# An expert kernel's first item: its rows turned by one-hot products straight from memory, and its item table computed between the up chunks

## What is computed

```python
h = h + mixed @ w_out[layer]
hn = rms_norm(h, norm_ffn_g[layer])
# moe_ffn(hn):
logits = xt @ router_w + router_b            # 512 x 32
top_vals, top_idx = lax.top_k(logits, 4)
gates = jax.nn.softmax(top_vals, axis=-1)
# tokens sorted by expert, in blocks of 128 rows of one expert each
gu = xblk @ w_gate_up[e] + b_gate_up[e]      # 1024 -> 2048
gate = jnp.minimum(gu[:, 0::2], 7.0)
lin = jnp.clip(gu[:, 1::2], -7.0, 7.0)
act = gate * jax.nn.sigmoid(1.702 * gate) * (lin + 1.0)
yb = act @ w_down[e] + b_down[e]             # 1024 -> 1024
y = zeros.at[buf_tok].add(yb * buf_gate[:, None])
return h + y
```

## Time and profile before

| | before |
|---|---|
| median of 3 executions | 1493.48 us |
| profiled execution: time / span in the profile | 1492.42 / 1490.8 us |
| mean granted TensorE clock over the span | 0.967 of 2.4 GHz |
| TensorE busy | 1436.0 us, 96% |
| VectorE busy | 1267.5 us, 85% |
| ScalarE busy | 1008.8 us, 68% |
| GpSimd busy | 262.1 us, 18% |
| DMA | 445.21 MB, mean 299 GB/s |

### The profile page before, as it was taken

The page is one execution under the profiler, slowest core; times in us unless marked ns, Lnnn a source line. Parts: engine busy times, 40 slices in busy tenths (PEclk is TensorE's granted clock), DMA queues, the critical chain, the costliest instruction groups (busy, mean ns, idle before and its releaser), DMA issues.

```text
span 1490.8 us, 20013 instructions
## 1 busy us (share of the span) xinstructions
PE 1436.0 (96%) x6500; PEld 1166.0 (78%) x6500; DVE 1267.5 (85%) x1020; ACT 1008.8 (68%) x971; POOL 262.1 (18%) x280
## 2 busy tenths in 40 slices
PE   6999989888999999999999999999999999999995
PEld 4887547775888888888888888888888888888884
DVE  4594865667999999999999999999999999999994
ACT  5346464334777777777777777777777777777773
POOL 3000000045011111221121111111211111221111
PEclk9999879958999999999999999999999999999998
DMA  7421001649999999999999999999999999999971
GB/s 241 154 79 57 1 1 65 260 122 301 355 384 361 385 371 366 370 375 374 373 364 366 371 367 367 381 356 368 386 359 382 365 356 368 378 371 365 370 290 21
DMA packets 96745, 445.21 MB, mean 299 GB/s; under 512 B 14863, under 2 KB 18975, under 8 KB 63888
## 3 DMA queue, kind: packets, MB, share of 16 engines
q1 hardware_dynamic: 82752, 421.82, 74.9%
q0 software_dynamic: 11392, 17.61, 4.9%
q10 hardware_dynamic: 2576, 5.46, 1.1%
HBM read 439.43 MB, written 22.43 MB: 310 GB/s over the span
## 4 chain that ended last, share of the span: by engine, by line
PE 94%; DVE 2%; ACT 1%; DMA 1%; issue 1%; SPq 0%; POOL 0%; ACTq 0%; POOLq 0%; DVEq 0%
PE psum L1257 27%; PE psum L1259 27%; PE psum L1258 27%; PE psum L1548 2%; PE psum L1573 2%; PE psum L1557 2%; PE psum L1355 2%; PE psum L1343 1%; DMA ring<-in_w_in 1%; PE psum L1357 1%; PE psum L1582 1%; PE psum L1477 1%; PE psum L1417 1%; DVE wlo L1160 0%; PE psum L1495 0%
## 5 line engine op out<-in xcount | busy, mean ns | idle before, releaser
L1160 DVE TENSOR_TENSOR wlo<-ring,whi 128x2048 fp32r<-128x2048 f32 x384 | 871.1, 2289 | 82.2 <-ACT whi L769 78.2
L769 ACT ACTIVATE whi<-ring 128x2048 fp32r<-128x2048 f32 x384 | 736.8, 1919 | 240.5 <-PE psum L1259 240.5
L1257 PE MATMUL psum<-whi,xT_hi 128*128 128x512 f32 x1024 | 402.9, 393 | 3.9 <-DVE xT_lo L1166 2.8
L1258 PE MATMUL psum<-whi,xT_lo 128*128 128x512 f32 x1024 | 399.8, 390 | 0.0
L1259 PE MATMUL psum<-wlo,xT_hi 128*128 128x512 f32 x1024 | 399.7, 390 | 0.0
L1257 PEld LDWEIGHTS psum<-whi,xT_hi 128*128 128x128 f32 x1024 | 193.2, 189 | 44.2 <-DVE xT_lo L1166 3.6
L1259 PEld LDWEIGHTS psum<-wlo,xT_hi 128*128 128x128 f32 x1024 | 192.9, 188 | 40.4
L1258 PEld LDWEIGHTS psum<-whi,xT_lo 128*128 128x128 f32 x1024 | 193.2, 189 | 39.0
L1257 PE MATMUL psum<-whi,aT_hi 128*128 128x512 f32 x512 | 202.5, 396 | 1.9 <-ACT y_sb L792 1.9
L1259 PE MATMUL psum<-wlo,aT_hi 128*128 128x512 f32 x512 | 199.7, 390 | 0.0
L1258 PE MATMUL psum<-whi,aT_lo 128*128 128x512 f32 x512 | 199.1, 389 | 0.0
(11 more groups left out here) (248 smaller groups left out, 1417.1 us busy)
## 6 DMA issues: line engine op xcount, KB each, us to landing
ring<-in_w_gate_up SPq DMA_DIRECT2D x256, 1024.0 KB, 7.6
ring<-in_w_down SPq DMA_DIRECT2D x128, 1024.0 KB, 6.9
ring<-in_w_in SPq DMA_DIRECT2D x10, 1024.0 KB, 11.5
ring<-in_w_out SPq DMA_DIRECT2D x4, 1024.0 KB, 5.0
h<-in_x SPq DMA_DIRECT2D x4, 512.0 KB, 5.5
hn_rows<-hn ACTq DMA_DIRECT2D x4, 512.0 KB, 3.0
out<-h ACTq DMA_DIRECT2D x4, 512.0 KB, 10.6
bias_rows<-rows_st SPq DMA_DIRECT2D x1, 1280.0 KB, 4.8
```

What stands on the lines that cost most here:

```text
L769: nc.scalar.activation(whi[:, hi_of(number), :], ring[:, slot(number), :], ACT.Copy).then_inc(hi_ready, 1)
L1160: TT(wlo[:, slot(number), :], ring[:, slot(number), :], whi[:, hi_of(number), :].bitcast(F32), ALU.subtract).then_inc(lo_ready, 1)
L1257: MM(o, s_hi, m_hi, start=first, stop=False)
L1258: MM(o, s_lo, m_hi, start=False, stop=False)
```

## The change

- Item 0's rows are no longer gathered. `first_rows(t)` multiplies the rows of hn, still in SBUF, by the one-hot matrix of expert 0's slots (`sel_rows`) and adds the four tiles up in PSUM banks 6 and 7: the rows come out chosen and turned. These are f32 products of 128x128, 8 a tile.
- The ranks use fp32r copies (`tri_r`, `ones_r`, `mask_r`): one pass.
- The first slots of items 1 and 2 (8 products in place of 12), the counts, the prefix, the item table and the turned gates are issued on TensorE between the up chunks 0 to 4 of item 0. VectorE's and ScalarE's lists are reordered to match; onehj is kept for all tiles, so that place(1) to place(3) and dense_gates can come later.
- ScalarE makes the high parts of chunks 0 and 1 between its gate exponentials.
- GpSimd gathers item 1 first, then writes all 16 scatters, then (after xgT_done) clears b_hl's upper half, then gathers item 2.

The core of the diff (address lines and renamings are left out):

```diff
@@ GpSimd
-                if isinstance(n, int) and n == 0:
+                if isinstance(n, int) and n == 1:
...
             nc.gpsimd.memset(xg[:, :], 0.0).then_inc(xg_cleared, 1)
             pool.wait_ge(slot0_ready, 1)
-            gather(0, slot0_i[:, 0:1])
+            gather(1, slot0_i[:, 1:2])
+            for t in range(T):
+                scatter_rows(t)
+            pool.wait_ge(xgT_done, 2)
             nc.gpsimd.memset(b_hl[2 * E:P, :].bitcast(F32), 0.0).then_inc(bhl_pad, 1)
-            scatter_rows(0)
-            scatter_rows(1)
-            gather(1, slot0_i[:, 1:2])
-            scatter_rows(2)
-            scatter_rows(3)
             gather(2, slot0_i[:, 2:3])
@@ ScalarE
             gates_exp(1)
+            hi_item(0, 0)
             gates_exp(2)
+            hi_item(0, 1)
...
             gates_exp(3)
...
-            for k in range(FIRST_HI):
-                hi_item(0, k)
-            act.wait_ge(gdT_done, 1)
-            nc.scalar.activation(gateT[:, :, :], bank(7)[0:E, :].rearrange("p (t c) -> p t c", t=T),
-                                 ACT.Copy).then_inc(gdT_evac, 1)
+            hi_item(0, 2)
             xgT_out(0)
+            hi_item(0, FIRST_HI)
+            hi_item(0, FIRST_HI + 1)
...
             nc.scalar.activation(b_hl[0:2 * E, :], b_raw[:, :], ACT.Copy).then_inc(bhl_hi, 1)
-            for k in range(FIRST_HI, UP):
+            for k in range(FIRST_HI + 2, UP):
                 hi_item(0, k)
+            act.wait_ge(gdT_done, 1)
+            nc.scalar.activation(gateT[:, :, :], bank(4)[0:E, :].rearrange("p (t c) -> p t c", t=T),
+                                 ACT.Copy).then_inc(gdT_evac, 1)
@@ VectorE
-                COPY(mask[:, t, 1:3, :], mask[:, t, 0:1, :].to_broadcast([P, 2, E])).then_inc(mask_ready, 1)
+                COPY(mask_r[:, t, :], mask[:, t, 0, :]).then_inc(mask_ready, 1)
+                COPY(mask[:, t, 1:3, :], mask[:, t, 0:1, :].to_broadcast([P, 2, E])).then_inc(mask_copied, 1)
...
             first_slot(0)
+            choose(1)
             dense_gates(0)
-            choose(1)
-            place(1)
+            choose(2)
             first_slot(1)
-            dense_gates(1)
-            choose(2)
-            place(2)
+            lo_item(0, 0)
             first_slot(2)
             choose(3)
             first_slot(3)
+            place(1)
+            place(2)
+            split_xgT(0)
+            dense_gates(1)
             place(3)
+            lo_item(0, 1)
             dve.wait_ge(slot0_done, 1)
...
+            flags()
+            dense_gates(2)
+            dense_gates(3)
+            lo_item(0, 2)
             places()
-            lo_item(0, 0)
+            lo_item(0, 3)
             items()
-            lo_item(0, 1)
-            split_xgT(0)
-            for k in range(2, UP):
+            for k in range(4, UP):
                 lo_item(0, k)
-                if k == FIRST_HI:
+                if k == 4:
@@ TensorE
+            def first_rows(t):
+
+                pe.wait_ge(sel0_ready, AHEAD * t + 1)
+                pe.wait_ge(hn_ready, t + 1)
+                if t == 0:
+                    pe.wait_ge(h1_done, T)
+                for half in range(2):
+                    for k in range(4):
+                        d = (half * 4 + k) * P
+                        ins = MM(bank(6 + half)[:, k * P:(k + 1) * P], hn[:, t, d:d + P], sel_rows[:, t, :],
+                                 start=(t == 0 and k == 0), stop=(t == T - 1 and k == 3))
+                    if t == T - 1:
+                        ins.then_inc(xgT_done, 1)
...
             ranks(0)
+            turn_hn(2)
             logits(1)
-            turn_hn(2)
             turn_hn(3)
+            logits(2)
             ranks(1)
-            logits(2)
             logits(3)
-            first_slots_of(0)
-            first_slots_of(1)
+            first_rows(0)
             ranks(2)
-            first_slots_of(2)
+            first_rows(1)
             ranks(3)
-            first_slots_of(3)
...
+            first_rows(2)
+            first_rows(3)
+            def counts():
+                pe.wait_ge(mask_copied, T)
+                pe.wait_ge(slot0_ready, 1)
...
-            pe.wait_ge(items_ready, 1)
-            pe.wait_ge(gdT_evac, 1)
-            transpose_xg(0)
             pe.wait_ge(xgT_ready, 2)
             for k in range(UP):
                 use_up(0, k, k)
+                if k == 0:
+                    for t in range(T):
+                        first_slots_of(t)
+                if k == 1:
+                    counts()
+                if k == 2:
+                    prefix()
+                if k == 3:
+                    item_table()
+                if k == 4:
+                    turn_gates()
             pe.wait_ge(bhl_ready, 1)
             pe.wait_ge(bhl_pad, 1)
             bias_up(0)
+            pe.wait_ge(items_ready, 1)
+            pe.wait_ge(gdT_evac, 1)
```

## The result

The changed kernel takes 1499.40 us (median of 5 executions, 1499.12 to 1502.54) against 1493.43 us for the kernel before (5 executions, 1489.54 to 1494.27). The ratio is 1.0046, with a 95% interval of 1.0035 to 1.0057: the change makes the kernel 6 us slower. The forecast was 1498.5, range 1493.5 to 1505.5. The profiled execution took 1499.24 us, 6.8 more than the profiled one of before (1492.42).

The account below looks back on a forecast made before the run. TensorE was taken to bound the kernel, with 94% of the span. 1490.8 - 11.4 (front) + 13.5 (up chunks) + 4.0 (clock) = 1496.9 us of span, with 1.6 outside it 1498.5; range 1493.5 to 1505.5.

Parts of the forecast that it names:

- Part 1: Way to the first up product: it starts at 313.5 instead of 324.93 us, gain 11.4 us (8.2 to 11.9).
- The factor of four: Rival in first_rows: f32 products four times as long as turnings, first up product at 333.5, 1518.5 us; chance 0.03.
- Part 2: Up chunks of item 0: VectorE's subtractions queued behind waits leave TensorE idle; eight chunks take 38.3 us instead of 24.75.
- Part 3: Gaps before up chunks: TensorE's clock falls twice, costing 4.0 us (1.6 to 6).
- Part 4: GpSimd's clearing of b_hl behind 16 scatters ends at 352.6 to 354.1, a floor of 2.8 to 4.3 us loss, adding nothing.
- Behind bias_up(0) nothing changes its order: After the up chunks: b_down products, item 1's turning and the loop take what they took before.
- The clock staying up: Rival in the gaps between chunks: clock stays at its upper level, only the clearing's floor binds, 1496.0 us; chance 0.15.
- The faster rival: Rival in the up chunks: subtractions done ahead cover the exchanges and the clearing does not bind, 1484.8 us; chance 0.07.
- the slow scatters: Rival on GpSimd: all scatters take 2.79 us, the clearing ends at 366, +16, 1508.5 us; chance 0.08.

Follow-up runs that it names:

- e8: Changed kernel with GpSimd's clearing of b_hl early and 12, 8 and 8 unused fill products in TensorE's three gaps: 1494.90 us, ratio 1.0018.
- e1: Changed kernel with VectorE's subtractions for chunks 2, 3 and 4 one place earlier, ahead of the waits: 1500.73 us, ratio 1.0047.
- e4: Changed kernel with 16, 10 and 10 unused fill products in TensorE's three gaps: 1499.66 us, ratio 1.0037.
- e2: e1 with GpSimd's clearing of b_hl ahead of the gather and the scatters: 1488.73 us, ratio 0.9974.
- e6: e2 with dense gates and b_hl's subtraction later, subtractions ahead of every exchange, turned gates behind chunk 6, ranks(2) ahead of first_rows(0): 1484.95 us, ratio 0.9942.
- e3: Changed kernel with early clearing; first slots, counts, prefix, item table and turned gates ahead of chunk 0; subtractions 1 to 7 behind places(): 1490.74 us, ratio 0.9981.
- e10: e6 with the ranks as f32 products of two records again: 1485.83 us, ratio 0.9963.
- e11: e3 with ranks(2) ahead of first_rows(0) and b_hl's subtraction behind the last chunk's: 1490.59 us, ratio 0.9973.

## Why the prediction was right, point by point

- **Part 1, the front: right in its working, 1 us off in its figure.** The first up product came at 312.46, released by xT_lo as said, against my 313.5; that is 0.5 us below the earliest time that I gave (313.0). The gain is 12.5 us, not 11.4. The last of first_rows ended at 311.05, against 311.1 in the working. The clock did come back in these f32 products: 16 records took 3.76 us in the first tile, 2.10 in the second, and the last two tiles 3.82 together, 1.9 each. 311.1 + 1.42 is 312.5: my 313.0 had 0.5 us in it that no row gives, and 313.5 another 0.5.
- **The factor of four: wrong, as the rows said.** At the lower clock 8 turnings take 1.94 us and 16 product records 3.76 us: a factor of 1.9. So the Trainium skill's statement in TensorE: Matmul & The Clock Gate, section Terms, that transpose mode is four times faster for FP32, is not borne out here. By it first_rows would have taken 31 us at the lower clock; at the lower clock one tile of four took 3.76, and all four took 9.7 with the clock back from the second tile on.
- **Part 2, the queue on VectorE: right in mechanism and in sum.** The stretches without a chunk were 4.99, 3.11 and 4.16 us before chunks 2, 3 and 4 (forecast 5.3, 3.2, 3.9), with the releasers named. The stage at the upper clock, which e8 shows, is 38.3 us: the forecast's figure. The fourth, before chunk 5, was 0.37 instead of 2.2 us: chunk 4 ran at the lower clock and so covered b_hl's subtraction; in e8 it is 1.98. e1 is the direct test of the cause: with the subtractions one place ahead, the stretches before chunks 2 and 4 are 0.6 us each, TensorE's own small products.
- **Part 3, the clock: right in size (4.1 against 4.0), wrong in count.** It fell three times, not twice, and cost 1.6, 2.5 and 1.7 us in chunks 2, 3 and 4, 5.8 together; the last is taken back by the gap before chunk 5 that it covers. The forecast had said of chunk 4 that it would be mostly hidden. Chunk 7 ended at 354.9 against 355.8.
- **Part 4, the clearing's floor: mis-sized for this kernel; it bound only in e1.** I put the clearing's end at 352.6 to 354.1; it was 346.8. (I also counted from a bias_up(0) at 349.84 before; it started at 349.68, so the floor as I worked it out was 2.9 to 4.4 us.) Only 4 of the 16 scatters were slowed (2.00 to 2.72 us, the others about 0.98: 20.7 us in all), since VectorE itself stood idle in the gaps. I had taken the durations of before, where 9 of the 16 were slowed. In e1, with dense subtractions, 7 were slowed, the clearing ended at 352.50, and with what its wait did to the clock it cost all that e1 had won. The exclusive lock that the Trainium skill states in SBUF — State Buffer, section "SBUF: two separate sides", agrees with this in one direction: the length of a scatter follows what VectorE does beside it. The other direction shows nowhere: beside a scatter VectorE's subtraction takes 2.27 to 2.29 us, as it does alone.
- **"Behind bias_up(0) nothing changes its order": true of the order, not of the time.** Four b_hl and 16 b_down records took 12.1 us instead of 10.8, which began at 349.68. The b_down records of before, from TensorE's timeline, answer to the 11.10 us of after:

```profile
350.68 9.83 PE L1582 MATMUL psum<-b_dn,gateT 32*128 32x512 f32 x16
```

  The clock falls in them in all twelve traces. How early it falls goes with their length, from 9.1 us in e4 to 14.0 in e1, where it was low from the start. That is the 1.3 us that the sum missed. The gain of part 1, 1.1 us more than forecast, made up for most of it: that the total came within 0.9 us is in this part luck.
- **The rivals.** The clock staying up was refuted (three falls). The faster rival was priced at 1484.8 on two conditions: VectorE gets the subtractions done ahead, and the clearing does not bind. e1 met the first, and the clearing then bound, at 352.5; on the scale of the kernel before, whose first rank product starts 1.1 us earlier, that is 351.4, against the 352.6 of that rival. e2 and e6 met both: 1488.7 and 1484.95. The change as it stands did not meet the condition. That e6 comes so near the price is in part luck: it moves the dense gates and b_hl's subtraction as well, and its stage is 26.6 us where the rival had 28.6; e2, which meets the two conditions and no more, has 31.6. For the slow scatters the rows show 2.75 us at most, not 2.79, and with 0.3 us between them the clearing would have ended at some 370, not 366; no run came near it.

What stays open: the executions of several kernels (e2, e3, e4, e10, e11) lie in two groups some 2 to 6 us apart, and the one profiled execution shows one of them. Part of it can lie ahead of everything that was changed. The lists of the engines up to the first rank product are the same in e8 and e6, yet e8's profiled execution, the shortest of its ten, reaches it at 284.91 and e6's at 289.65. The windows views of e8 and of e6 show the granted clock at 0.89 and at 0.80 in the attention:

```profile
210.00:240.00 30.00, 30.00 (x107) 18.34 (x107) 15.17 (x23) 8.54 (x28) 0.00 (x0) 0.89 0.00 1
```
```profile
210.00:240.00 30.00, 27.16 (x91) 16.26 (x92) 15.91 (x26) 11.79 (x36) 0.00 (x0) 0.80 0.00 1
```

In the other traces the same holds: 0.89 goes with a first rank product at 285.35 (e4), 0.85 with 287.3 and 287.5 (before, after), 0.82 and 0.83 with 288.4 to 288.7, 0.80 with 289.56 (e2). That the two groups of one kernel differ by this is a guess, since no kernel was profiled in both, and it doesn't reach the longer executions of e4.

## What to carry to other kernels

Before moving a chain of exchanges between two engines in between the big work, write down each engine's queue and look at what stands behind each wait: here three subtractions of 2.28 us, issued one place too late, left TensorE idle for 10.1 us and cost some 4 us more by the clock; issued one place earlier, and with what can wait put behind them, they left 0.2 us. Moving something out of the way uncovers what it hid, and then the next thing: the wait for the gather showed only once the table had moved (5.4 us of idle time, 3.8 at item 1), the clearing only once the gaps were closed (9.4 us), so edits are to be tried in pairs before one of them is dismissed. A busy share of 96% on both sides of the change says nothing of it; the idle time in front of one line, with its releaser, says it.

## What the runs showed of the hardware

- **A TensorE that is busy all the time can still be granted the lower clock.** In the changed kernel, 359 to 367 us, it was busy for 8.00 of 8.00 us with f32 products of 32 rows, at 0.50. In 345 to 355 us, with 128x512 products, it had 0.99. The 16 products of 32 rows took from 9.1 (e4) to 14.0 us (e1).
- **Products whose result nobody uses hold the clock.** In e8, 28 of them in gaps of 5.0, 3.1 and 3.8 us kept it at 1.00, where it had fallen to 0.50 three times. The stage became 4.1 us shorter, though the gaps were nearly as long as in the changed kernel (5.0, 3.1 and 4.2 us).
- **With f32 products of 128x128 it came back.** In first_rows of the changed kernel it went from 0.50 at 301 to 304 us to 0.93 in 304 to 306, three rank products of 32 columns among them, where the small products of before, without a pause too, had stayed at 0.50.
- **A scatter's length is set by its neighbour.** It is 0.97 to 1.06 us alone and 1.87 to 3.17 where VectorE's large subtraction is under way as the scatter starts or begins within 0.03 us of it, over all kernels here. A scatter that runs already when the subtraction begins keeps its 0.98 (322.31 in the changed kernel, the subtraction 322.54). In the changed kernel all four long ones end 0.85 us after a subtraction does (three of a weight, one of b_hl), so the sum over 16 scatters can't be taken from another kernel's trace: 20.7 us in after, 24.8 in e1.
